# A chunked state-space scan: the exponent clamped by a ScalarE rectifier, and the next step's decays weighed before the output chain

## What is computed

```python
a_cum = jnp.cumsum(da, axis=-1)
causal = jnp.tril(jnp.ones((L, L), dtype=bool))
decay = jnp.exp(jnp.where(causal, a_cum[..., :, None] - a_cum[..., None, :], -jnp.inf))
cb = jnp.einsum('bclgn,bcsgn->bcgls', cc, bc)
y_diag = jnp.einsum('bcgls,bcgjls,bcsgjp->bclgjp', cb, decay, xd)
...
y_off = jnp.einsum('bclgn,bcgjpn,bcgjl->bclgjp', cc, prev, jnp.exp(a_cum))
return (y_diag + y_off).reshape(bsz, seq, SSD_N_HEADS, SSD_HEADDIM)
```

## Time and profile before

| | before |
|---|---|
| median of three runs | 1262.43 us |
| the profiled execution, its own time | 1260.18 us |
| its span, first to last instruction | 1258.4 us |
| TensorE busy | 1173.2 us (93%) |
| VectorE busy | 390.8 us (31%) |
| ScalarE busy | 265.6 us (21%) |
| mean granted clock of TensorE, share of full speed | 0.994 |

### The profile page before, as it was taken

One profiled execution on the slowest core, in us unless ns is written; L12 is line 12 of the kernel. 1 busy time (PEld: TensorE's weight loads), 2 busy tenths in 40 slices (PEclk: granted clock), 3 DMA queues, 4 the chain that ended last, 5 costly groups with the idle time before them and its releaser, 6 DMA issues.

```text
span 1258.4 us, 15354 instructions
## 1 busy us (share of the span) xinstructions
PE 1173.2 (93%) x6172; PEld 617.0 (49%) x6172; DVE 390.8 (31%) x706; ACT 265.6 (21%) x409; POOL 7.5 (1%) x27
## 2 busy tenths in 40 slices
PE   7999999999999999999898899899999998999996
PEld 6998887898633433333333333334433333343432
DVE  5887676646311211111111111212211111122112
ACT  6555444445210101010100001101101011011102
POOL 1000000000000000000000000000000000000000
PEclk9999999999999999999999999989999999999999
DMA  9453313488799999999999999999999999999996
GB/s 325 165 201 135 134 69 133 149 320 321 293 409 427 429 428 428 430 428 429 429 429 428 428 430 428 429 427 428 429 427 430 428 429 428 392 432 427 431 422 258
DMA packets 55655, 454.28 MB, mean 361 GB/s; under 512 B 6397, under 2 KB 6565, under 8 KB 30533
## 3 DMA queue, kind: packets, MB, share of 16 engines
q1 hardware_dynamic: 55440, 453.74, 87.1%
q10 hardware_dynamic: 180, 0.07, 0.0%
HBM read 452.74 MB, written 1.05 MB: 361 GB/s over the span
## 4 chain that ended last, share of the span: by engine, by line
PE 53%; DMA 42%; DVE 2%; SPq 1%; issue 1%; DVEq 1%; ACT 1%; ACTq 0%
DMA ring<-in_moe_w_down 41%; PE ps L889 13%; PE ps L913 11%; PE ps L564 3%; PE ps L566 3%; PE ps L565 3%; PE ps L923 2%; PE ps L865 2%; PE ps L579 2%; PE ps L581 2%; PE ps L580 2%; PE ps L698 1%; DMA wring<-in_ssd_w_in 1%; PE ps L900 1%; SPq L435 1%
## 5 line engine op out<-in xcount | busy, mean ns | idle before, releaser
L913 PE MATMUL ps<-ring,wring 128*64 128x512 f32 x960 | 216.5, 597 | 52.2 <-DMA ring<-in_moe_w_down 52.2
L889 PE MATMUL ps<-ring,wring 128*64 128x512 f32 x1024 | 223.3, 594 | 0.0
L913 PEld LDWEIGHTS ps<-ring,wring 128*64 128x64 f32 x960 | 65.0, 137 | 191.8 <-issue 112.3
L1033 ACT ACTIVATE wring<-ps 128x512 f32<-128x512 f32 (+2 forms) x101 | 52.4, 535 | 502.4 <-PE ps L889 431.4
L1736 DVE COPY wring<-ps 128x512 f32<-128x512 f32 x32 | 22.1, 691 | 405.9 <-PE ps L889 405.9
L889 PEld LDWEIGHTS ps<-ring,wring 128*64 128x64 f32 x1024 | 72.1, 137 | 139.7 <-issue 139.6
L1744 DVE TENSOR_TENSOR wring<-ps,bguT 128x512 f32<-128x512 f32 x64 | 41.2, 686 | 299.7 <-PE ps L900 299.7
L889 PE MATMUL ps<-mid,wring 128*64 128x512 f32 x512 | 115.8, 605 | 1.0 <-DVE wring L1744 1.0
L1033 ACT ACTIVATE ysb<-ps 128x512 f32<-128x512 f32 x36 | 21.5, 598 | 270.2 <-PE ps L913 249.5
L889 PEld LDWEIGHTS ps<-mid,wring 128*64 128x64 f32 x512 | 36.1, 139 | 69.5 <-issue 69.5
L865 PEld LDWEIGHTS ps<-wring 128*128 128x128 f32 x480 | 55.8, 191 | 23.5 <-issue 23.5
(11 more groups left out here) (317 smaller groups left out, 1405.8 us busy)
## 6 DMA issues: line engine op xcount, KB each, us to landing
ring<-in_moe_w_gate_up SPq DMA_DIRECT2D x64, 2048.0 KB, 22.7
ring<-in_moe_w_down SPq DMA_DIRECT2D x60, 2048.0 KB, 25.5
mid<-in_moe_w_gate_up SPq DMA_DIRECT2D x32, 2048.0 KB, 23.5
wring<-in_moe_w_gate_up SPq DMA_DIRECT2D x16, 2048.0 KB, 26.4
hs<-in_moe_w_gate_up SPq DMA_DIRECT2D x16, 2048.0 KB, 27.9
wring<-in_ssd_w_in SPq DMA_DIRECT2D x10, 2048.0 KB, 8.4
wring<-in_xa_w_kv SPq DMA_DIRECT2D x4, 2048.0 KB, 8.1
wring<-in_ssd_w_out SPq DMA_DIRECT2D x4, 2048.0 KB, 7.8
```

What stands on the lines that cost most here:

```text
L889: last = mm(ps[a][SLOTS * half:SLOTS * (half + 1), :], xs[:, m, c % 2, :], w[:, kk, c0:c0 + 512], start=s + kk == 0, stop=s + kk == GP)
L913: last = mm(ps[D_BANK][SLOTS * half:SLOTS * (half + 1), :], act[:, k, :], w[:, kk, 512 * half:512 * (half + 1)], start=k == 0, stop=k == K ...
L1033: return nc.scalar.activation(out_, in_, func, **kw)
```

## The change

The products L656, their two operands and the semaphore behind these are taken out. ScalarE turns the exponent over and rectifies it (two instructions of 128x512, PSUM to `mt`), drains, and takes the exponential of the negated result in place, in one instruction of 128x1024. So exp(min(x, 0)) stands where exp(x - 1e30 above the diagonal) stood.

On VectorE the weighing becomes a function `weigh(i)` and the rows for the state a function `state_rows(g)`. Step 0's are done ahead of the loop. In iteration i the weighing of step i + 1 stands ahead of the output chain of step i, where it stood behind it. `w_lo` of steps 1, 3 and 4 goes behind the output chain.

```diff
-        diag, above = part(lo_ring, 3840, 3968), part(lo_ring, 3968, 4096)
...
-                    pe.wait_ge(diag_ok, 1)
                 for b in range(2):
-                    mm(ps[2 + b][:, :], lrow[:, i % 2, :], rall[:, c, 4 * b:4 * b + 4, :], start=True, stop=False)
-                    mm(ps[2 + b][:, :], diag, above.unsqueeze(1).to_broadcast([P, 4, P]), start=False, stop=True)
+                    mm(ps[2 + b][:, :], lrow[:, i % 2, :], rall[:, c, 4 * b:4 * b + 4, :], start=True, stop=True)
...
                 for b in range(2):
-                    last = fn(mt[:, i % 2, 4 * b:4 * b + 4, :], ps[2 + b][:, :].rearrange("p (h l) -> p h l", h=4), ACT.Exp)
-                last.then_inc(exp_ok, 1)
+                    fn(mt[:, i % 2, 4 * b:4 * b + 4, :], ps[2 + b][:, :].rearrange("p (h l) -> p h l", h=4), ACT.Relu,
+                       scale=-1.0)
+                act_.drain()
+                fn(mt[:, i % 2, :, :], mt[:, i % 2, :, :], ACT.Exp, scale=-1.0).then_inc(exp_ok, 1)
...
-            dve.wait_ge(z_ps, 8)
-            v.tensor_copy(diag, ident)
-            v.tensor_scalar(above, tri, -1.0, 1e30, ALU.add, ALU.mult).then_inc(diag_ok, 1)
...
+            def state_rows(g):
                 gs, hs = slice(GW_ * g, GW_ * (g + 1)), slice(HPG * g, HPG * (g + 1))
-                if c == 0:
-                    dve.wait_ge(dec_ok, 1)
-                    v.tensor_tensor(by_head(xde), by_head(xd[:, 0, gs]), spread(dec[:, 0, hs]),
-                                    ALU.mult).then_inc(xde_ok, 1)
+                if g:
+                    dve.wait_ge(main_ps, 2 * g - 1)
+                v.tensor_tensor(by_head(xde), by_head(xd[:, 0, gs]), spread(dec[:, 0, hs]),
+                                ALU.mult).then_inc(xde_ok, 1)
+
+            def weigh(i):
                 dve.wait_ge(exp_ok, i + 1)
                 dve.wait_ge(cb_ok, i + 1)
                 v.scalar_tensor_tensor(out=mt[:, i % 2, :, :], in0=mt[:, i % 2, :, :], scalar=1.0,
                                        in1=cbm[:, i % 2, :].unsqueeze(1).to_broadcast([P, HPG, P]), op0=ALU.min,
                                        op1=ALU.mult).then_inc(mt_ok, 1)
-                for n, half in KV_SPLIT[i]:
-                    w_lo(n, half)
+
+            decays(0)
+            dve.wait_ge(dec_ok, 1)
+            state_rows(0)
+            weigh(0)
+            for i in range(2 * GROUPS):
...
+                if i == 0:
+                    for n, half in KV_SPLIT[0]:
+                        w_lo(n, half)
                 if i + 1 < 2 * GROUPS:
                     decays(i + 1)
+                    if c == 1:
+                        state_rows(g + 1)
+                    weigh(i + 1)
                 dve.wait_ge(main_ps, i + 1)
...
                 v.tensor_tensor(yb[:, c, gs], yb[:, c, gs], zs[:, c, gs], ALU.mult).then_inc(u_ok, 1)
+                if i:
+                    for n, half in KV_SPLIT[i]:
+                        w_lo(n, half)
```

More of the change, by code:

```diff
@@ L226, in build @@
                              "dec_ok"))
-        acx_ok, rall_ok, l_ok, diag_ok = sem("acx_ok"), sem("rall_ok"), sem("l_ok"), sem("diag_ok")
+        acx_ok, rall_ok, l_ok = sem("acx_ok"), sem("rall_ok"), sem("l_ok")
         (prep_ps, cb_ok, exp_ok, mt_ok, main_ps, st_ok, xde_ok, y_read, u_ok, ssu_ok, kv_ps,
@@ L1545, in decays @@
                     group_row(i + 2)
-            decays(0)
-            for i in range(2 * GROUPS):
-                g, c = i // 2, i % 2
+            def state_rows(g):
                 gs, hs = slice(GW_ * g, GW_ * (g + 1)), slice(HPG * g, HPG * (g + 1))
-                if c == 0:
-                    dve.wait_ge(dec_ok, 1)
-                    v.tensor_tensor(by_head(xde), by_head(xd[:, 0, gs]), spread(dec[:, 0, hs]),
-                                    ALU.mult).then_inc(xde_ok, 1)
+                if g:
[3 more added lines that the diff above has]
+            def weigh(i):
                 dve.wait_ge(exp_ok, i + 1)
@@ L1559, in _ @@
                                        op1=ALU.mult).then_inc(mt_ok, 1)
-                for n, half in KV_SPLIT[i]:
-                    w_lo(n, half)
+            decays(0)
[3 more added lines that the diff above has]
+            for i in range(2 * GROUPS):
+                g, c = i // 2, i % 2
+                gs, hs = slice(GW_ * g, GW_ * (g + 1)), slice(HPG * g, HPG * (g + 1))
+                if i == 0:
+                    for n, half in KV_SPLIT[0]:
+                        w_lo(n, half)
                 if i + 1 < 2 * GROUPS:
                     decays(i + 1)
+                    if c == 1:
+                        state_rows(g + 1)
+                    weigh(i + 1)
                 dve.wait_ge(main_ps, i + 1)
```

## The result

The changed kernel takes 1254.46 us, the median of five runs (1253.78 to 1255.93), against 1261.38 us for the kernel before, the median of five (1260.73 to 1262.75). The three runs with the median of 1262.43, from which the forecast started, are among these five. The ratio is 0.9945, with a 95% interval of 0.9934 to 0.9957: 6.9 us faster, between 5.4 and 8.3. The profiled execution took 1253.78 us with a span of 1251.9, where the working had 1253.8.

What follows compares the result with a forecast made beforehand. The weight stream bounds the expert loop, TensorE the scan before it. Savings of 3.7 + 2.9 = 6.6 us, taken as 6.4 with allowance for the last step, gave 1262.43 - 6.4 = 1256.0 us; range 1254.8 to 1259.4.

Steps and rivals of the forecast that it cites:

- The mask's products: TensorE in the scan: two products fewer in each of eight preps, 0.23 us each, gain 3.7 us.
- The stalls: TensorE's scan waiting for VectorE's weighing: three stalls of 0.91 us plus a little in step 7, gain 2.9 us.
- `diag` and `above`: Mask operands built on VectorE ahead of the scan: removing them gains nothing, at most 0.2 us.
- Rectifiers, drain, exponential: ScalarE in each step: 1.08 + 0.08 + 1.05 = 2.21 us, making the exponential 1.13 us later than before.
- The circle: Exponential, weighing, output chain, square, next rectifiers: 12.47 us per pair of steps, against TensorE's 12.42.
- slack at scan 7: Bank 5 must be read before scan 7: due 5.24 us after prep 7, ready at 5.12, slack 0.1 us.
- The stream: Weight loads of the expert loop: they start earlier by as much as scan 7, so scan gains reach the end.
- The rival in which it hides the gain: Expert loop's weight stream alone sets the end, time stays 1262.4 us; chance 0.08, including gain lost elsewhere.
- the one with the tables: ScalarE reloads tables for rectifier and exponential each step, 2.57 us more, 1273.0 us; chance 0.05, including similar new waits.
- the one with the circle as the bound: In the scan, a longer loop of waits across engines sets the pace, gain only 2.6 to 5.8 us; chance 0.26.
- the last step of the working: From profiled execution to median: 1253.8 us profiled, median 2.25 us above it, hence 1256.0 us.
- the last step, which I had held to be tight: Step 7 of the scan: something allowed for its tightness, lowering the expected gain from 6.5 to 6.4 us.

Runs made afterwards that it cites:

- the clamp alone: Against the kernel before: mask products removed, ScalarE rectifies, drains and exponentiates, VectorE keeps the old order; 1259.10 us, ratio 0.9987.
- the move alone: Against the kernel before: only VectorE's new order, mask products and two exponentials from PSUM kept; 1258.36 us, ratio 0.9979.
- the lengthened circle: Changed kernel plus one more drained rectifier of 128x512 per step, on values it does not change; 1258.93 us, ratio 0.9984 to before.
- the cut circle: Changed kernel plus the same extra drained rectifier per step, with each square taken one step later; 1254.78 us, ratio 0.9949 to before.
- the seven experiments: Changed kernel timed again, its two parts singly, extra rectifier with and without later squares, clamp on VectorE, first quarter before prep 0; ratios 0.9945 to 0.9987.
- The two comparisons: Changed kernel against the kernel before, timed twice without edit between: 1254.46 us, ratio 0.9945, then 1254.32 us, ratio 0.9952.
- the two lengthened kernels: Changed kernel plus an extra drained rectifier per step, squares unmoved (1258.93 us) or one step later (1254.78 us).

## Why the prediction was right in its working and wrong in its number

**The mask's products**, 3.7 us: 0.46 us per step, as measured in the period (6.67 to 6.21 us). Right; and the clamp alone showed that 1.4 us of them depend on the move.

**The stalls**, 2.9 us: the move alone gave 2.84. Right. (Its profiled span is only 1.2 us under that of the kernel before; most of what is missing lies behind the issue, see below.)

**`diag` and `above`**, nothing: prep 0 waited 0.45 us in the changed kernel, for ScalarE, and 0.41 us before. Right: the gate activation was what it waited for. The profile of the kernel before names L1538, but that had ended 0.44 us before prep 0 began, and with it gone the wait is as long:

```profile
137.40 0.22 DVE L1538 TENSOR_SCALAR lo_ring<-cst 128x128 fp32r<-128x128 f32 x1
```

**Rectifiers, drain, exponential**, 1.08 + 0.08 + 1.05 = 2.21 us: measured from 152.08 to 153.23 + 1.06, 2.21 us. Right.

**The circle**, 5.56 + 6.91 = 12.47 us: 12.35 by the estimate from the lengthened circle. The mechanism is right, and the cut circle shows that it is a circle. But by the forecast it was 0.05 us longer than TensorE's pair, and by the estimate it is 0.06 shorter, so that TensorE sets the pace. Its slack at scan 7 was mis-sized as well, 0.1 us forecast, 0.5 measured (the rectifiers of step 7 were 0.7 and not 1.0 us late). Most of that is `w_lo`: I let `w_lo` of step 4 push the weighing of step 6 by 0.3 us. It pushed it by nothing, as in the last two steps `decays` has no L1503 left to issue; the exponential ended at 179.12 and the weighing began at 179.15.

**The stream** moves along with the scan: in all nine profiles the issue stands 151.79 to 151.92 us behind scan 7. The rival in which it hides the gain has fallen. So has the one with the tables, and the one with the circle as the bound: with 0.7 us more per step it is one, in the changed kernel it is not.

**The number.** What failed is the last step of the working, from the profiled execution to the median: "the median lies 2.25 us above it". For the changed kernel it lies 0.68 us above. That 2.25 was the difference between one execution and a median of three, and I carried it over as if it belonged to the kernel. In the seven experiments the median lies between 0.54 us below the profiled execution (the move alone) and 0.81 above it (the clamp alone). Of the 1.5 us between 1256.0 and 1254.46 this term explains all (2.25 - 0.68 = 1.57). The same 1.57 can be split another way. The base was 1.05 us too high, for 1262.43 became 1261.38 with two more runs, and 1261.1 to 1261.5 in the larger series. The gain between medians was 6.9 us and not 6.4, 0.5 more; 0.1 of this is the last step, which I had held to be tight (6.51 us in the scan), and the cause of the rest is open.

The sum against the profiled execution came out (1253.8 forecast, 1253.78 measured), but that it came out to 0.02 us is luck. Of the 6.51 us won in the scan 6.22 had arrived at the issue, since prep 0 started 0.42 us later and the stretch from scan 7 to the issue was 0.13 shorter; and the stretch behind the issue gave 0.3. The change does not touch that one, and it differs between profiles by 1.6 us: 1258.4 - 346.34 = 912.1 us before, 1251.9 - 340.12 = 911.8 after, 1257.2 - 343.78 = 913.4 with the move alone, the other six between the last two.

The range did not allow for this. By the largest gain that it names, 7.2 us, its low end would be 1255.2; it stands at 1254.8, and the working doesn't say where the 0.4 come from. Either way nothing in it stands for the scatter of a median of three runs.

Whether the gain between medians is 6.5 or 6.9 us stays open. The two comparisons (5.4 to 8.3 and 4.3 to 7.8) hold both.

## What to carry to other kernels

Two parts of a change that act on one step don't add up where one engine's chain hides the other's savings: take the stall away first, or with it, and count a saving only in the steps in which its engine is the one that is late. When work is moved ahead of a wait, write down the circle that it closes over all engines and compare its length with that of the bound engine; here one more 0.7 us instruction per step set scan 7 back by 4 us, and moving one instruction out of the circle took that loss away. Make the sum against the profiled execution, but take the distance of a median from it as scatter, and give the range at least that much at both ends.

## What the runs showed of the hardware that was not expected

A rectifier needed no table load beside the exponential: ten loads before and ten after. A clamp of 128x1024 floats out of PSUM held VectorE for 1.13 us (one instruction) and ScalarE for 1.15 us (two, with a drain behind them). And a short hold of ScalarE, put down to issue, came once in each of the two lengthened kernels, 0.35 us in step 5; the changed kernel has none there. Its cause wasn't looked for.
